# Two of sixteen k tiles of an up-projection as seven block products, with the weight sums made by accumulating DMAs

## The reference

```
def conv_ffn(x, norm2_g, w_up, conv_w, conv_b, w_down):
    h = rms_norm(x, norm2_g)
    u = h @ w_up                       # (256, 2048) @ (2048, 11008)
    u = causal depthwise conv, width 3, over the tokens, + conv_b
    gate, val = jnp.split(u, 2, axis=-1)
    return x + (jax.nn.silu(gate) * val) @ w_down
```

## Time and profile before

| | |
|---|---|
| timed runs, median (lowest to highest) | 1038.23 us (1037.99 to 1040.0) |
| profiled execution, whole time | 1039.86 us |
| its span, first to last instruction | 1038.1 us |
| granted TensorE clock, mean | 1.000 |
| PE busy | 1031.2 us (99%) |
| DVE busy | 801.3 us (77%) |
| ACT busy | 799.7 us (77%) |
| POOL busy | 21.1 us (2%) |
| DMA | 221.04 MB, mean 213 GB/s |
| up-projection: first and last start of line 712 | 370.4 and 815.5 us |

### The profile page before, as it was taken

The page is one execution under the profiler, slowest core; times in us unless marked ns, Lnnn a source line. Parts: engine busy times, 40 slices in busy tenths (PEclk is TensorE's granted clock), DMA queues, the critical chain, the costliest instruction groups (busy, mean ns, idle before and its releaser), DMA issues.

```text
span 1038.1 us, 16517 instructions
## 1 busy us (share of the span) xinstructions
PE 1031.2 (99%) x5278; PEld 931.9 (90%) x5278; DVE 801.3 (77%) x1354; ACT 799.7 (77%) x1406; POOL 21.1 (2%) x27
## 2 busy tenths in 40 slices
PE   9999999999999999999999999999999999999998
PEld 8999999999988888888888888888889988888887
DVE  7788888878766655577776776777768799989988
ACT  7776676888858885879788788797887789856753
POOL 0101010000000000000000000000000000000000
PEclk9999999999999999999999999999999999999999
DMA  9666777777766666666565565665656757656664
GB/s 351 240 199 212 216 239 229 222 252 227 249 229 201 205 194 201 204 213 201 189 218 195 193 221 190 213 203 188 216 187 190 232 182 233 201 200 218 203 203 162
DMA packets 81437, 221.04 MB, mean 213 GB/s; under 512 B 20312, under 2 KB 24544, under 8 KB 81248
## 3 DMA queue, kind: packets, MB, share of 16 engines
q1 hardware_dynamic: 81232, 220.07, 65.0%
q10 hardware_dynamic: 144, 0.20, 0.1%
HBM read 214.32 MB, written 5.91 MB: 212 GB/s over the span
## 4 chain that ended last, share of the span: by engine, by line
PE 87%; DVE 8%; DMA 2%; ACT 1%; issue 1%; SPq 0%; DVEq 0%; ACTq 0%
PE ps L714 14%; PE ps L713 14%; PE ps L712 14%; PE ps L501 7%; PE ps L503 7%; PE ps L502 7%; PE ps L741 4%; PE ps L743 4%; PE ps L742 4%; DVE w_lo L1314 3%; PE ps L691 3%; PE ps L693 3%; PE ps L692 3%; DMA raw<-in_wrest 2%; PE ps L523 1%; DVE sums_lo_t L1883 1%
## 5 line engine op out<-in xcount | busy, mean ns | idle before, releaser
L1314 DVE TENSOR_TENSOR w_lo<-raw,w_hi 128x1024 fp32r<-128x1024 f32 (+2 forms) x406 | 457.1, 1131 | 186.3 <-ACT w_hi L838 184.4
L838 ACT ACTIVATE w_hi<-raw 128x1024 fp32r<-128x1024 f32 (+2 forms) x406 | 393.4, 977 | 145.3 <-PE ps L714 53.1
L712 PE MATMUL ps<-w_hi,xs 128*128 128x512 f32 (+1 forms) x704 | 263.4, 374 | 0.0
L713 PE MATMUL ps<-w_lo,xs 128*128 128x512 f32 (+1 forms) x704 | 263.4, 374 | 0.0
L714 PE MATMUL ps<-w_hi,xs 128*128 128x512 f32 (+1 forms) x704 | 263.4, 374 | 0.0
L501 PE MATMUL ps<-w_hi,xs 128*128 128x384 f32 (+1 forms) x496 | 164.9, 332 | 0.1
L502 PE MATMUL ps<-w_lo,xs 128*128 128x384 f32 (+1 forms) x496 | 161.8, 326 | 0.0
L503 PE MATMUL ps<-w_hi,xs 128*128 128x384 f32 (+1 forms) x496 | 161.8, 326 | 0.0
L712 PEld LDWEIGHTS ps<-w_hi,xs 128*128 128x128 f32 x704 | 133.1, 189 | 17.2
L713 PEld LDWEIGHTS ps<-w_lo,xs 128*128 128x128 f32 x704 | 133.1, 189 | 17.2
L714 PEld LDWEIGHTS ps<-w_hi,xs 128*128 128x128 f32 x704 | 133.1, 189 | 17.2
(11 more groups left out here) (231 smaller groups left out, 1139.1 us busy)
## 6 DMA issues: line engine op xcount, KB each, us to landing
raw<-in_wrest SPq DMA_DIRECT2D x278, 512.0 KB, 4.0
raw<-in_win SPq DMA_DIRECT2D x117, 384.0 KB, 3.6
raw<-in_wrest SPq DMA_DIRECT2D x16, 384.0 KB, 3.1
p_scratch<-pdT SPq DMA_DIRECT2D x14, 192.0 KB, 2.9
p_read<-p_scratch SPq DMA_DIRECT2D x56, 48.0 KB, 2.8
xtok<-in_xtok SPq DMA_DIRECT2D x4, 512.0 KB, 13.2
xv<-in_xtok SPq DMA_DIRECT2D x4, 512.0 KB, 5.6
raw_ahead<-in_w SPq DMA_DIRECT2D x5, 392.0 KB, 8.1
```

The costliest lines, as they stand in the source:

```text
L712: pe.matmul(o, xh, wh, start=(k == 0), stop=False, skip_group_check=True)
L713: pe.matmul(o, xh, wl, start=False, stop=False, skip_group_check=True)
L838: act.activation(slot(w_hi, s, w), slot(raw, s, w), ACT.Copy).then_inc(hi_ready, 1)
L1314: dve.tensor_tensor(slot(w_lo, s, w), slot(raw, s, w), f32(slot(w_hi, s, w)), ALU.subtract).then_inc(split_done, 1)
```

## The change

In the batches 1 to 8 (`UP_BATCHES`) the k tiles 8 and 9 (`UP_SEVEN`) are no longer two pieces of 12 matmuls. Seen as a product of 2x2 blocks (two token halves x two k tiles, times two k tiles x two column halves), they are made by seven block products of three matmuls, with sums of blocks on both sides, and results that are combined afterwards.

- **Pieces.** The two pieces become four: `left` (the gate half of k tile 8, 512 columns), `lower` (k tile 9, 1024), and `two` and `more`, 1024 columns each of sums of the four blocks. A batch with sums has 18 pieces (`UP_LONG`), numbered j = 0 to 17 below: 0 to 7 as before, 8 to 11 the four new ones, 12 to 17 the k tiles 10 to 15. All loads go through the same ring.
- **Weight sums.** They are made in DRAM (`t_scratch`) by DMAs that POOL issues, `build_sums`: for each of eight sets three plain copies and three accumulating DMAs, 1 MB by each kind, each one behind a wait for the one before. Set q starts no earlier than `piece_used` = `OUT0` + 8 + 16q. SP loads `two` and `more` from there, and waits for the set before the first.
- **Activation sums.** They are made once, in batch 0: two additions of 256 columns, a subtraction of 256 and an addition and a subtraction of 128 on DVE (`h_sums`), a rounding of 512 columns on ACT (`h_sums_hi`), and the subtraction that leaves the low parts, 512 columns, on DVE (`h_sums_lo`).
- **Products.** Three of the seven add into the batch's own banks, four go to banks of the other parity, which batch nb-1 has been evacuated from by then. ACT copies the first of these out (`take_first`), DVE combines the four in four additions (`up_sums`) into `x1sq` and `x1f`, ACT multiplies both by `r2` (`scale_sums`).
- **Evacuation.** For batches with sums it goes from ACT to DVE (`evacuate_sums`): bank times `r2` plus the combined sum, four instructions behind the first split of the next batch. Both transposes follow behind its second split.
- **Order.** What follows which split on ACT and DVE is given by two tables, by the piece j of the batch behind whose split of piece j+4 it stands.
- Apart from this, the semaphores of two norms are merged.

The numbers and the two tables:

```diff
@@ -35,10 +35,13 @@
 BATCH = 4
 FULL = FT // BATCH
 LAST = FT - FULL * BATCH
-OUT_PIECES, UP_PIECES, DOWN_PIECES = KT * KT // 8, (FULL + 1) * KT, FT * KT // 8
+UP_SEVEN, UP_BATCHES = (8,), (1, 8)
+UP_SUMS = len(UP_SEVEN) * (UP_BATCHES[1] - UP_BATCHES[0] + 1)
+UP_LONG, UP_EXTRA = KT + 2 * len(UP_SEVEN), 2 * UP_SUMS
+OUT_PIECES, UP_PIECES, DOWN_PIECES = KT * KT // 8, (FULL + 1) * KT + UP_EXTRA, FT * KT // 8
 OUT0 = IN_PIECES
 UP0 = OUT0 + OUT_PIECES
-UP_LAST0 = UP0 + FULL * KT
+UP_LAST0 = UP0 + FULL * KT + UP_EXTRA
 DOWN0 = UP0 + UP_PIECES
 UW, LW = BATCH * P, LAST * P
...
 ADD_AT = 42
+UP_ACT = dict(late_silu=5, moves=(3, 3, 4, 4, 6, 8, 10, 10), first=9, scale=(14, 16), taps=(11, 12, 15, 16), silu=(13, 17, 17))
+UP_DVE = dict(late_taps=(3, 6), late_gate=(4, 8), evacuate=(0, 0), turn=(1, 1), sums=(9, 10),
+              taps=((11, 12), (14, 14), (16, 16)), gate=(15, 16))
 OUT_ORDER = [(0, b) for b in range(7)] + [(1, 0), (0, 7)] + [(1, b) for b in range(1, 8)] + [(blk, b) for blk in (2, 3) for b in range(8)]
 
 
```

The pieces and their loads on SP:

```diff
+        def up_parts(nb):
+
+            if not with_sums(nb):
+                return [("piece", k) for k in range(KT)]
+            parts = []
+            for k in range(KT):
+                if k in UP_SEVEN:
+                    parts += [(kind, k) for kind in ("left", "lower", "two", "more")]
+                elif k - 1 not in UP_SEVEN:
+                    parts.append(("piece", k))
+            return parts
+
...
+                    s = up_at(nb, par, j) % RING
+                    sp.wait_ge(split_done, up_first(nb) + (j - RING + 1))
+                    if kind in ("two", "more"):
+                        q = (nb - UP_BATCHES[0]) * n + UP_SEVEN.index(k)
+                        c = 0 if kind == "two" else PW
+                        if kind == "two":
+                            sp.wait_ge(t_built, 96 * (q + 1))
+                        sp.dma_start(slot(raw, s), t_d[q * P:(q + 1) * P, c:c + PW]).then_inc(raw_landed[s], 16)
+                        continue
+                    w = BLOCK if kind == "left" else PW
+                    row = (UP0 - IN_PIECES + nb * KT + k + (kind == "lower")) * P
+                    sp.dma_start(slot(raw, s, w), wrest_d[row:row + P, 0:w]).then_inc(raw_landed[s], 16)
+
+            rest_pieces(OUT0 + 8, UP0 + KT, PW, 0)
+            for nb in range(UP_BATCHES[0], UP_BATCHES[1] + 1):
+                up_pieces(nb, nb % 2)
+            rest_pieces(UP_LAST0 - KT, UP_LAST0, PW)
             rest_pieces(UP_LAST0, DOWN0, 2 * LW)
             rest_pieces(DOWN0, ALL_PIECES, PW)
             for g in range(ALL_PIECES // RING * RING, ALL_PIECES):
                 sp.wait_ge(split_done, g - RING + 1)
-                sp.dma_start(slot(raw, g % RING), wrest_d[(g - IN_PIECES) * P:(g - IN_PIECES + 1) * P, :]
-                             ).then_inc(raw_landed[g % RING], 16)
+                at = g - IN_PIECES - UP_EXTRA
+                sp.dma_start(slot(raw, g % RING), wrest_d[at * P:(at + 1) * P, :]).then_inc(raw_landed[g % RING], 16)
 
             def store(count, o, m, blk, at=0, n=BLOCK):
```

The products on PE:

```diff
+                def a(kk, m):
+                    return [xs[:, (k + kk) * 2 * S + m * S + h * P:(k + kk) * 2 * S + m * S + (h + 1) * P] for h in range(2)]
+
+                def a_sum(i):
+                    return [h_sum(n, i, h) for h in range(2)]
+
+                def b(jj, half):
+                    at = up_at(nb, par, j + jj) % RING
+                    return [weave(slot(t, at, BLOCK, half * BLOCK)) for t in (w_hi, w_lo)]
+
+                def product(to, x, w, start=False, stop=False):
+                    pe.matmul(bank(to), x[0], w[0], start=start, stop=False, skip_group_check=True)
+                    pe.matmul(bank(to), x[0], w[1], start=False, stop=False, skip_group_check=True)
+                    return pe.matmul(bank(to), x[1], w[0], start=False, stop=stop, skip_group_check=True)
+
+                if first:
+                    pe.wait_ge(u_evac, nb * 4)
+                if isinstance(nb, int) and nb == UP_BATCHES[0]:
+                    pe.wait_ge(h_lo, n + 1)
+                pe.wait_ge(split_done, up_first(nb) + (j + 1))
+                product(shared[0], a(0, 0), b(0, 0), first, last).then_inc(piece_used, 1)
+                pe.wait_ge(split_done, up_first(nb) + (j + 2))
+                product(own[0], a(1, 0), b(1, 0))
+                product(own[1], a_sum(3), b(1, 1)).then_inc(piece_used, 1)
+                pe.wait_ge(split_done, up_first(nb) + (j + 3))
+                product(shared[2], a_sum(1), b(2, 0), first, last)
+                product(shared[3], a_sum(0), b(2, 1), first, last).then_inc(piece_used, 1)
+                pe.wait_ge(split_done, up_first(nb) + (j + 4))
+                end = product(shared[1], a_sum(2), b(3, 0), first, last)
+                if last:
+                    end.then_inc(c_ended, 1)
+                product(own[2], a(1, 1), b(3, 1)).then_inc(piece_used, 1)
+
             def up_batch(nb, par, w=UW):
 
                 if isinstance(nb, int) and nb < 2:
                     pe.wait_ge(x1_done, 4 * (nb + 1))
                 else:
                     pe.wait_ge(u_evac, nb * 4 - 4)
-                for k in range(KT):
+                if not isinstance(nb, int) or UP_BATCHES[0] < nb <= UP_BATCHES[1] + 1:
+                    pe.wait_ge(c_summed, nb * 4 - 4)
+                for j, (kind, k) in enumerate(up_parts(nb)):
                     if isinstance(nb, int) and nb == 0:
                         pe.wait_ge(h2_ready, k + 1)
-                    up_piece(nb, k, UP_BANKS[par], w)
+                    if kind == "piece":
+                        up_piece(nb, par, k, j, w)
+                    if kind == "left":
+                        up_seven(nb, par, k, j)
 
             for nb in range(3):
```

New work on ACT:

```diff
+            def take_first(nb, par):
+
+                act.wait_ge(c_ended, nb)
+                act.wait_ge(u_evac, nb * 4)
+                act.activation(c_tile(0, 0), bank(UP_BANKS[1 - par][0]), ACT.Copy).then_inc(c_first, 1)
+
+            def scale_sums(nb, m):
+
+                act.wait_ge(c_summed, nb * 4)
+                act.activation((x1sq, x1f)[m][:], (x1sq, x1f)[m][:], ACT.Copy, scale=r2[:, m:m + 1]).then_inc(c_scaled, 1)
+
```

New work on DVE:

```diff
+            def up_sums(nb, par, step):
+
+                m6, m5, m7 = [bank(UP_BANKS[1 - par][i]) for i in (1, 2, 3)]
+                if step == 0:
+                    dve.wait_ge(c_first, nb)
+                    dve.wait_ge(u_evac, nb * 4)
+                    dve.tensor_tensor(c_tile(1, 1), m6, c_tile(0, 0), ALU.subtract).then_inc(c_summed, 1)
+                    dve.wait_ge(c_summed, nb * 4 - 3)
+                    dve.tensor_tensor(c_tile(0, 1), m5, c_tile(1, 1), ALU.add).then_inc(c_summed, 1)
+                if step == 1:
+                    dve.tensor_tensor(c_tile(1, 0), m7, c_tile(1, 1), ALU.subtract).then_inc(c_summed, 1)
+                    dve.wait_ge(c_summed, nb * 4 - 1)
+                    dve.tensor_tensor(c_tile(1, 1), c_tile(0, 1), m7, ALU.subtract).then_inc(c_summed, 1)
+
+            def evacuate_sums(pb, m, par):
+
+                dve.wait_ge(piece_used, up_first(pb) + UP_LONG)
+                dve.wait_ge(c_scaled, pb * 2 + (m - 1))
+                dve.wait_ge(u_turned, pb * 2)
+                for gv in range(2):
+                    at = (2 * m + gv) * UW
+                    dve.scalar_tensor_tensor(out=ut[:, at:at + UW], in0=bank(UP_BANKS[par][2 * m + gv]), scalar=r2[:, m:m + 1],
+                                             in1=c_tile(m, gv), op0=ALU.mult, op1=ALU.add).then_inc(u_evac, 1)
+
```

The building of weight sums on POOL:

```diff
+            def build_sums(q):
+
+                nb, n = q // len(UP_SEVEN) + UP_BATCHES[0], q % len(UP_SEVEN)
+                at = (UP0 - IN_PIECES + nb * KT + UP_SEVEN[n]) * P
+                upper, both = wrest_d[at:at + P, :], wrest_d[at:at + 2 * P, :].rearrange("(k p) c -> p k c", k=2)
+                lower = wrest_d[at + P:at + 2 * P, :]
+                row = t_d[q * P:(q + 1) * P, :]
+
+                def block_(i, n=1):
+                    return row[:, i * BLOCK:(i + n) * BLOCK]
+
+                pool.dma_start(block_(0, 2), upper).then_inc(t_built, 16)
+                pool.wait_ge(t_built, 96 * q + 16)
+                pool.dma_start(block_(0, 2).rearrange("p (k c) -> p k c", k=2), both[:, :, BLOCK:PW], accum_op=ALU.add,
+                               max_dma_last_dim=4096).then_inc(t_built, 16)
+                pool.wait_ge(t_built, 96 * q + 32)
+                pool.dma_start(block_(2), block_(0)).then_inc(t_built, 16)
+                pool.wait_ge(t_built, 96 * q + 48)
+                pool.dma_start(block_(2), lower[:, BLOCK:PW], accum_op=ALU.add, max_dma_last_dim=4096).then_inc(t_built, 16)
+                pool.wait_ge(t_built, 96 * q + 64)
+                pool.dma_start(block_(3), block_(2)).then_inc(t_built, 16)
+                pool.wait_ge(t_built, 96 * q + 80)
```

(7 more changed lines are left out.)

173 lines of the change are left out of this document (147 added, 26 removed).

## The result

The changed kernel takes 1051.38 us (median of four runs, 1048.73 to 1054.3) against 1038.28 for the kernel before: 1.0123 of it, interval 1.0088 to 1.0159, 13.1 us more. The forecast was 1034.0, in a range up to 1046. Rival 2, slower by contention at 1045 to 1058, has the right sign and size. Its account of the cause is only half of what the runs show.

The account below looks back on a forecast made before the run. PE's issue of matmuls was taken to bound the up-projection. From 1038.23 us, 5.2 went for 24 fewer matmuls and 1.0 came back for later loads, ACT and DVE adding nothing: 1034.0 us, range 1032.6 to 1046.

Parts of the forecast that it names:

- Rival 2: Accumulating DMAs hold the DMA engines, so loads land after 6.1 us or more wherever sets are built: 1045 to 1058; chance 0.16.
- What bounds the kernel, and the matmuls: Up-projection: PE's matmul issue sets its time; 24 fewer matmuls at 0.216 us save 5.2 us.
- The sums for ACT and DVE: Engine work per batch with sums: DVE 36.9 and ACT 35.8 of 40.8 us, so both fit.
- rival 4: DVE's evacuations or additions cost more than the upper bound; pieces 13 to 15 late, 1 us per batch: 1041; chance 0.04.
- One batch, from PE's start on it: One up-projection batch followed piece by piece through PE, ACT, DVE and loads; PE never waits, so no loss.
- the narrowest place: Piece 13 of a batch: split by DVE at 26.4, wanted by PE at 27.8; spare 1.4 us, 1.0 more in landing.
- How much later do SP's own loads land?: SP's loads beside POOL's transfers: half land at 4 to 6 us; 0.2 us lost in each of five batches, 1.0 in all.
- The tolerance of 5 us: By the batch followed, all loads may take 5 us for nothing; at 5.5 pieces 11 and 13 are late, 0.5 us each.
- The set of DMAs: POOL's chain of six DMAs per set takes 37 us; all eight sets stay hidden up to 50 us each.
- Rival 3: A set takes over 50 us and SP waits for it: 1048 at 52 us, 1112 at 60; chance 0.06.
- Rival 1: Loads land at 5.5 to 6.5 us; PE waits 3.1 to 7.3 us at pieces 11 and 13: about 1038; chance 0.14.
- a sign against its narrow place: In the trace after: landings of 6 us with no wait of PE would prove the narrow-place account wrong.

Follow-up runs that it names:

- narrow moves and no building: Changed kernel with plain weights loaded instead of built sums, and each ACT move from batch 3 on copying a quarter of its blocks: 1034.01 us, 0.9962 of before.
- Without building: Changed kernel without POOL's building of weight sums or SP's wait for them; SP loads plain weights of the same size: 1037.87 us, 0.9987 of before.
- the building alone: Kernel before, with POOL building the same eight sets of sums at the same places and nobody reading them: 1039.36 us, 1.0005 of before.
- narrow moves: Changed kernel, POOL's building of sums included, with each ACT move from batch 3 on copying a quarter of its blocks: 1043.15 us, 1.005 of before.
- small accumulation: Changed kernel with the 512 KB accumulating DMA of each set adding only 32 of its 512 columns: 1048.06 us, 1.0094 of before.
- other order: Changed kernel, building included, with other numbers in the two order tables: ACT moves later, DVE takes taps closer together: 1051.52 us, 1.0119 of before.
- early building: Changed kernel with all sets of sums started in the attention, after the first 9 heads' pieces are used: 1053.33 us, 1.0133 of before.
- the large one first: Changed kernel, complete, with POOL from set 1 on holding each set's 512 KB accumulating DMA until batch q starts: 1050.19 us, 1.0116 of before.

## Why the prediction was wrong

- **What bounds the kernel, and the matmuls: right.** 24 fewer, 0.216 us each. With narrow moves and no building a batch takes 40.8 us and the kernel 4.0 us less than before.
- **The sums for ACT and DVE: right.** 36.9 and 35.8 us forecast; windows of 37.14 and 36.60 in batch 3. The evacuation takes what was forecast too (0.66 us apart; the row has the duration). So rival 4 is out.

```profile
L2023 DVE SCALAR_TENSOR_TENSOR ut<-ps,r,x1sq x16: 740/743/747, 459.0 to 760.1; 128x512 f32<-128x512 f32 x16
```

- **"One batch, from PE's start on it": the step that failed first.** It found 1.4 us to spare in the engines at the narrowest place and none short. Measured, the cycle is short by 0.6 us at piece 11, even with loads that land as before. The working had batch nb-1 evacuated by 7.7 us and ACT's moves start at 11.5 (10.56 and a split). Without building, DVE is done with what the batch before left over at 3.9 us in batch 5 (it starts at 575.38), the four evacuations are through at 8.9, and the moves start at 12.5. In batch 3 (start 493.20) the three come at 3.3, 8.3 and 11.9, and that batch loses nothing. DVE's evacuations and ACT's moves, batch 3, then DVE's evacuations, batch 5 (its moves are shown above, 587.85):

```profile
498.74 1.40 DVE L2022 SCALAR_TENSOR_TENSOR ut<-ps,r,x1sq 128x512 f32<-128x512 f32 x2
...
505.05 2.61 ACT L1304 ACTIVATE uT<-utT 32x512 f32<-32x512 f32 x4 [0.23 <-DVE utT L1918]
...
581.54 1.40 DVE L2022 SCALAR_TENSOR_TENSOR ut<-ps,r,x1sq 128x512 f32<-128x512 f32 x2
```

From 12.5 on ACT has 6.5 us of moves and 3.1 of splits and silu before it can round piece 11, at 22.0. DVE has it split at 24.3, and PE wants it at 24.0. Checked against PE at piece 13 only, this looked fine: the narrow place is where PE's pieces are short (0.65 and 1.3 us) while a split still costs 0.96 on ACT and 1.14 on DVE. The term stood at nothing in the sum, and it is worth 3.7 us of the 5.2 gained. In the changed kernel the moves start at 13.5 in batches 2, 3, 4 and 6.
- **"How much later do SP's own loads land?": the step that cost most.** Landings "at 4 to 6 us" were right for the median. The start was already too good: 3.5 us is batch 5 alone, while batches 2 to 5 of before have 3.3/4.2/5.3. The tolerance of 5 us was taken from the batch worked before, so it was too high by the same error. And the 1.0 us to spare in the landing was counted from piece 13's load going out at 19.5; it went out at 21.8 in batch 4. The term stood in the sum at 1.0 us; building costs 11.6 in the profiles and 13.5 in the timed runs. The two terms together were 1.0 us and measured 15.3.
- **The set of DMAs: right.** 37 us forecast, 38.6 to 41.5 measured from the issue of its first DMA to the landing of its last, limit 50. SP never waited for one. Rival 3 is out. That the parts add up so well is in part luck: 37 was six times the one landing of a load beside another, and the six DMAs of a set have medians from 4.4 to 10.6 us.
- **Rival 1** (the narrow place leaks within 0.2%) names the right place, and the kernel without building lies in its range with 1037.87 us. But there the leak comes with loads as before and at piece 11, not with loads of 5.5 us at 11 and 13. With building the loss of 15.3 us is twice the 7.3 that it allowed.
- **Rival 2, right in sign and size.** Its condition, landings over 6.1 us wherever a set is built, holds for the worst loads and not for the median, and its premise that contention suffices was disproved by the building alone. The chance of 0.16 was too low, as I see it because room on ACT and DVE and lateness of loads were judged one after the other, each by a margin that the other had used up.
- **The clock** stood in no step. A wait of 2.6 us was followed by 3.1 us at 1.2 GHz.

Batch 5 of the changed kernel loses only 0.4 us at a DMA share of 0.87, with 6 of its 17 loads of weights above 6.1 us. That is close to what the prediction named as a sign against its narrow place. The rows offer a reason: while PE lost 4.4 us at piece 13 of batch 4, DVE and ACT went on with their lists, so in batch 5 the evacuations are through at 8.0 us and the moves start at 11.5, as in the forecast. No run tests it.

Still open: how the 9 us that building costs even with narrow moves (4.9 in the profiles) divide between DVE, whose 37 us are untouched there, and the landing itself. A kernel with room on DVE alone was not run, nor one in which loads are late without POOL. No version ran faster than the kernel before and did its work. The nearest thing to a bound is the 1034.0 us of the kernel with narrow moves and no building, which does neither the whole convolution nor the sums: about 5 us less on ACT per batch, and sums that don't come through DRAM beside the loads. No kernel with its full work has shown it.

## What to carry to other kernels

Work out the lead of a ring at the pieces that are shortest for the engine that sets the pace, not where the spare is asked about last; a full list on a feeding engine (ACT without a pause between two splits) can already be a wait. Background DMAs are free only for loads with a margin: test them in the kernel as it is and in the kernel with the new work, as either alone may show nothing. Judge landings by their tail, not their median.

## What the runs showed of the hardware

Accumulating DMAs within DRAM are slow: 512 KB land in 10.6 us in the median (8.2 to 12.1), 256 KB in 6.7 to 7.2, where plain ones take 5.0 and 4.4 to 4.9. POOL spends 1.17 us on issuing the former:

```profile
L2279 POOL DMA_DIRECT2D t_scratch<-in_wrest x8: 1167/1170/1213, 313.4 to 597.5; - x8
...
DMA to landing us min/median/max: 8.2/10.6/12.1
```

Beside them a 512 KB load of SP takes up to 9.4 us (up to 5.3 in the same batches before). One issued at 478.3, 0.9 us behind an accumulation, landed after 7.9 us, 3.3 us ahead of it (489.5). So it is slowed and not held until the accumulation is through, which agrees with the Trainium skill (DMA: Bandwidth & Descriptors, section "Queues, rings and completion order": the DMA engines take turns between queues).

PE's granted clock fell to 0.50 beside six single waits: 2.61 us (changed kernel), 1.95 (small accumulation), 1.89 (other order), and 2.61, 2.94 and 4.39 (early building). It stayed at 1.00 through six others of 1.20 to 1.72 us (1.23, 1.20, 1.31, 1.69, 1.37 and 1.72, in the changed kernel, the large one first, the other order and the early building). In the first three cases the stretch that follows costs 1.5 to 2.7 us on top of the wait.
